# Half-size products summed in PSUM by TensorE, with ScalarE copies between, in the first layer's projection of a two-layer encoder

## The reference, cut to what matters

```python
hmod = rms_norm(x, norm_pre) * (1.0 + scale) + shift
u = jnp.dot(hmod, w_in)
x_a, g_a, q, k, v, g_b = jnp.split(u, EVEN_SPLITS, axis=-1)
xc, new_buf = causal_dwconv(x_a, conv_buf, conv_w)          # 4 taps
h, h_last = rg_lru(xc + conv_b, h0, w_a, b_a, w_x, b_x, lam)
y_a = h * jax.nn.silu(g_a)
...                                                          # window attention gives y_b
y = jnp.dot(jnp.concatenate([y_a, y_b], axis=-1), w_out)

# rg_lru, per channel, with r and i two sigmoid gates of small block products:
log_a = -LRU_C * r * softplus(-lam);  a = exp(log_a)
gated_x = sqrt(-expm1(2.0 * log_a)) * (i * xf)
h[t] = a[t] * h[t-1] + gated_x[t]
```

## Time and profile before

| | us |
|---|---|
| median of 3 runs (lowest, highest) | 1354.24 (1353.94, 1354.58) |
| the profiled execution's own time | 1355.17 |
| its span in the trace | 1353.0 |
| TensorE busy, share of the span | 1322.2, 98% |
| VectorE busy | 847.0, 63% |
| ScalarE busy | 434.6, 32% |
| GpSimd busy | 331.3, 24% |

### The profile page before, as it was taken

The page is one execution under the profiler, slowest core; times in us unless marked ns, Lnnn a source line. Parts: engine busy times, 40 slices in busy tenths (PEclk is TensorE's granted clock), DMA queues, the critical chain, the costliest instruction groups (busy, mean ns, idle before and its releaser), DMA issues.

```text
span 1353.0 us, 28616 instructions
## 1 busy us (share of the span) xinstructions
PE 1322.2 (98%) x11800; PEld 917.9 (68%) x11800; DVE 847.0 (63%) x1940; ACT 434.6 (32%) x1044; POOL 331.3 (24%) x450
## 2 busy tenths in 40 slices
PE   5999999999999999999999999999999999999997
PEld 4677776666655554667877788877788777875543
DVE  2747874355453375684885858868588585782246
ACT  4213443344431232521423314234142241432211
POOL 1023200010013232623312323124232242212352
PEclk9999999999999999999999999999999999999999
DMA  9521006002035522121112012120121200441124
GB/s 368 231 69 36 8 33 278 1 1 79 3 131 169 195 92 100 22 73 30 69 36 68 34 36 93 38 70 35 34 85 44 74 35 33 137 149 26 44 85 169
DMA packets 63769, 112.03 MB, mean 83 GB/s; under 512 B 34832, under 2 KB 39176, under 8 KB 62104
## 3 DMA queue, kind: packets, MB, share of 16 engines
q1 hardware_dynamic: 63640, 110.21, 24.3%
HBM read 91.79 MB, written 18.40 MB: 81 GB/s over the span
## 4 chain that ended last, share of the span: by engine, by line
PE 87%; DVE 7%; DMA 3%; POOL 1%; issue 1%; ACT 1%; SPq 0%; DVEq 0%; POOLq 0%; ACTq 0%
PE psum L1136 82%; PE psum L1139 4%; DMA mem<-x 1%; DVE mem L2971 1%; DVE mem L2782 1%; DVE mem L3296 1%; DMA mem<-x_dram 1%; DMA y<-mem 0%; DVE mem L3062 0%; DVE mem L3173 0%; DVE mem L2951 0%; POOL mem L958 0%; DVE mem L2788 0%; ACT mem L2095 0%; DVE mem L3050 0%
## 5 line engine op out<-in xcount | busy, mean ns | idle before, releaser
L1136 PE MATMUL psum<-mem 32*32 32x32 f32 (+12 forms) x11216 | 1261.6, 297 | 7.3 <-DMA mem<-modw 1.4
L1136 PEld LDWEIGHTS psum<-mem 128*128 128x128 f32 (+6 forms) x11216 | 851.2, 141 | 388.3 <-issue 199.5
L2971 DVE SCALAR_TENSOR_TENSOR mem<-mem 128x576 f32<-128x576 f32 (+1 forms) x126 | 106.2, 843 | 0.0
L1139 PE MATMUL psum<-mem 128*128 128x128 f32 (+1 forms) x584 | 83.7, 281 | 16.6 <-ACT mem L1935 13.7
L1139 PEld LDWEIGHTS psum<-mem 128*128 128x128 f32 (+1 forms) x584 | 69.3, 146 | 39.1 <-issue 19.3
L2286 ACT ACTIVATE mem<-mem 128x128 f32<-128x128 f32 x72 | 22.0, 305 | 127.7 <-DVE mem L3221 74.5
L2752 DVE TENSOR_TENSOR mem<-mem,psum 128x512 f32<-128x512 f32 x28 | 19.2, 687 | 42.5 <-PE psum L1136 40.5
L1015 POOL COPY mem<-mem 128x3 f32<-128x3 f32 x24 | 8.9, 370 | 148.8 <-DVE mem L2929 71.1
L2172 ACT ACTIVATE mem<-psum 128x288 f32<-128x288 f32 x28 | 11.4, 407 | 104.0 <-PE psum L1136 104.0
L2064 ACT ACTIVATE mem<-mem 128x256 f32<-128x256 f32 x72 | 35.5, 495 | 26.4 <-DVE mem L2705 26.4
L2182 ACT ACTIVATE mem<-mem 128x576 f32<-128x576 f32 (+1 forms) x42 | 32.7, 779 | 28.0 <-DVE mem L2949 28.0
(11 more groups left out here) (260 smaller groups left out, 1268.1 us busy)
## 6 DMA issues: line engine op xcount, KB each, us to landing
mem<-modw SPq DMA_DIRECT2D x12, 2048.0 KB, 11.2
mem<-w SPq DMA_DIRECT2D x44, 512.0 KB, 4.4
mem<-x SPq DMA_DIRECT2D x10, 512.0 KB, 4.6
x_dram<-mem SPq DMA_DIRECT2D x9, 512.0 KB, 2.9
mem<-row_dram SPq DMA_DIRECT2D x8, 576.0 KB, 5.0
mem<-x_dram SPq DMA_DIRECT2D x9, 512.0 KB, 3.7
mem<-wout SPq DMA_DIRECT2D x1, 4096.0 KB, 15.1
mem<-gs SPq DMA_DIRECT2D x8, 512.0 KB, 3.6
```

What stands on the lines that cost most here:

```text
L1136: return pe.matmul(*a, **k)
L1139: return pe.transpose(out, in_, ident[0:n, 0:n])
L2971: x = dve.scalar_tensor_tensor(cvm, U1[:, m, lo + j:hi + j], CW[:, 3 * g + ORDER[m], j:j + 1], cvm, ALU.mult, ALU.add)
```

## The change

The seven products and their operands stay. What changes is where they are added, who empties the banks, and in which order the engines of the loop come to it:

- The products are made in the order 1, 2, 6, 5, 7, 4, 3. Products 1, 6, 7 and 4 accumulate in one bank (`start` is false for 6, 7 and 4), products 5 and 3 in bank 4 or 5, and product 2 stands alone.
- ScalarE copies the running sum out after each of 1, 6, 7 and 4 (p1, u2, u3, c21): 8 copies in a pair in place of 2. TensorE adds the next product onto a bank only after the copy. u2, u3, u4 and c21 are no longer VectorE's work; c11, c22 and c12 stay, 6 instructions in a pair in place of 14.
- On VectorE the whole convolution of the next tile, and c11, stand ahead of the wait for the square root; c22 stands between the last product and the scan; the gates of c12 stand at the head of `chain`.
- On ScalarE the two tanh of c12 stand at the head of the turn, ahead of the six tanh that empty banks 6 and 7; the copies of p1 stand ahead of the exponential, those of u2 ahead of the square root, those of u3 and c21 between the tanh of the gates.

The diff's core:

```diff
-STEP = {"1": 0, "6": 2, "2": 4, "7": 6, "5": 8, "4": 10, "3": 12}
+STEP = {"1": 0, "2": 2, "6": 4, "5": 6, "7": 8, "4": 10, "3": 12}
+ADD, ADDS0 = {"c11": 0, "c22": 2, "c12": 4}, 6
+COPY, COPIES0 = {"p1": 0, "u2": 2, "u3": 4, "c21": 6}, 8
 def pair_bank(p, step):
-    return 2 * ((ROLE[step] + p) % 3)
+    return 4 if step in "53" else 2 * (1 - p % 2) if step == "2" else 2 * (p % 2)
...
# TensorE, pair
-                               start=(k == 0), stop=(k == HALF - 1))
+                               start=(k == 0 and step in "125"), stop=(k == HALF - 1),
+                               skip_group_check=(step in "6743"))
...
                 for j in range(2):
+                    pe.wait_ge(sem("st_cp"), copied_to(p, "p1", j))
                     part("6", j, S2, 0, T2, 0, lo(j))
                 for j in range(2):
+                    if p:
+                        pe.wait_ge(sem("st_add"), added_to(p - 1, "c12", j))
...
+                    part("5", j, w2, 0, T1, 0, lo(j))
                 for j in range(2):
-                    pe.wait_ge(sem("st_cp"), 2 * p + j + 1)
+                    pe.wait_ge(sem("st_cp"), copied_to(p, "u2", j))
                     part("7", j, S3, 0, T3, 0, lo(j))
...
                 for j in range(2):
-                    pe.wait_ge(sem("st_add"), STEPS * p + ADD["c11"] + j + 1)
+                    pe.wait_ge(sem("st_cp"), copied_to(p, "u3", j))
                     part("4", j, w2, HALF, T4, 0, lo(j))
                 pe.wait_ge(sem("s_made"), 4 * p + SUMS["s4"])
                 for j in range(2):
-                    pe.wait_ge(sem("st_add"), STEPS * p + ADD["u3"] + j + 1)
+                    pe.wait_ge(sem("st_add"), added_to(p, "c22", j))
                     part("3", j, S4, 0, HT, HALF, hi(j))
...
# ScalarE, lru
+                if m:
+                    gate_tanh(m - 1, "c12", U2c)
                 for i in range(6):
                     wait(act, sem("l_mm"), 6 * m + i + 1)
...
+                if m < LM - 1:
+                    copied(m + 1, "p1")
                 c.mark(act.activation(la, tr, ACT.Exp, ...))
                 act.activation(lw_, tr, ACT.Tanh, ...).then_inc(sem("l_a"), 1)
                 if m < LM - 1:
-                    copied(m + 1)
-                if m:
-                    gate_tanh(m - 1, "c12", U2c)
+                    copied(m + 1, "u2")
                 wait(act, sem("l_w"), m + 1)
...
-                for name, src in (("c11", P1c), ("c22", V22), ("c21", U3c)):
-                    gate_tanh(m, name, src)
+                gate_tanh(m, "c11", P1c)
+                copied(m + 1, "u3")
+                gate_tanh(m, "c22", V22)
+                copied(m + 1, "c21")
+                gate_tanh(m, "c21", U3c)
...
# VectorE, added, chain and lru
-            ADDS = {"u2": (P1c, U2c, "cp"), "c11": (P1c, P1c, "cp"), "u3": (U2c, U3c, "u2"),
-                    "c22": (U3c, V22, "u3"), "u4": (U2c, U2c, "u2"), "c21": (U3c, U3c, "u3"),
-                    "c12": (U2c, U2c, "u4")}
+            ADDS = {"c11": (P1c, "p1"), "c22": (V22, "u3"), "c12": (U2c, "u2")}
...
                 for j in range(2):
                     dve.wait_ge(sem("st_mm"), STEPS * p + STEP[FROM[name]] + j + 1)
+                    dve.wait_ge(sem("st_cp"), copied_to(p, after, j))
...
+                if m:
+                    gates(m - 1, "c12", U2c)
                 dve.wait_ge(sem("l_a"), m + 1)
...
-                if m:
-                    gates(m - 1, "c12", U2c)
                 if m < LM - 1:
-                    added(m + 1, "u2")
+                    conv0(m + 1)
+                    added(m + 1, "c11")
                 dve.wait_ge(sem("l_sq"), m + 1)
                 c.sync()
                 c.mark(dve.scalar_tensor_tensor(lg, ti, 0.5, lw_, ALU.mult, ALU.mult))
+                if m < LM - 1:
+                    added(m + 1, "c22")
...
                 p = m + 1
-                added(p, "c11")
-                conv0(m + 1, 0)
-                added(p, "u3")
-                conv0(m + 1, 1)
                 gates(m, "c11", P1c)
-                added(p, "c22")
-                added(p, "u4")
                 gates(m, "c22", V22)
-                added(p, "c21")
                 gates(m, "c21", U3c)
                 dve.wait_ge(sem("g_ev"), G_PAIR * m + OUTS["c21"] + 2)
                 dve.scalar_tensor_tensor(YT[:, m], lh, 0.5, YT[:, m], ALU.mult, ALU.mult
                                          ).then_inc(sem("l_y"), 1)
                 added(p, "c12")
```

More of the change, by code:

```diff
@@ L1270, in pair @@
                 for j in range(2):
-                    freed(j, 0, "u4")
+                    if p:
+                        pe.wait_ge(sem("st_add"), added_to(p - 1, "c11", j))
+                    else:
+                        pe.wait_ge(sem("xa_ev"), j + 1)
                     part("1", j, w1, 0, HT, 0, lo(j))
+                for j in range(2):
+                    if p:
+                        pe.wait_ge(sem("st_cp"), copied_to(p - 1, "c21", j))
+                    else:
+                        pe.wait_ge(sem("xa_ev"), 2 + j + 1)
+                    part("2", j, w1, HALF, HT, HALF, lo(j))
                 pe.wait_ge(sem("s_made"), 4 * p + SUMS["s2"])
@@ L1312, in gates, with freed @@
                     pe.wait_ge(sem(f"w0_in{q}"), 16 * m + 48)
-                    project(m, q, "g_mm", lambda n: pe.wait_ge(
-                        sem("st_add"), STEPS * (PAIRS - 1) + LAST_FREE[3 * q + n]))
+                    def freed(n):
+                        j = (3 * q + n) % 2
+                        if 3 * q + n >= 4:
+                            pe.wait_ge(sem("st_add"), added_to(PAIRS - 1, "c12", j))
+                        elif 3 * q + n < 2:
+                            pe.wait_ge(sem("st_add"), added_to(PAIRS - 1, "c11", j))
+                        else:
+                            pe.wait_ge(sem("st_cp"), copied_to(PAIRS - 1, "c21", j))
+                    project(m, q, "g_mm", freed)
             tiles(LM, gates)
@@ L1954, in constants, with copied @@
                 c.mark(act.activation(ltmp[:, 0], ltmp[:, 1], ACT.Tanh))
-            def copied(p):
+            COPIED = {"p1": (P1c, "c11"), "u2": (U2c, "c12"), "u3": (V22, "c22"), "c21": (U3c, "c21")}
+            def copied(p, name):
+                dst, last = COPIED[name]
                 for j in range(2):
-                    wait(act, sem("st_mm"), STEPS * p + STEP["1"] + j + 1)
+                    wait(act, sem("st_mm"), STEPS * p + STEP[FROM[name]] + j + 1)
                     if p >= 2:
[L1961 to L1964, removed]
+                        wait(act, sem("g_ev"), G_PAIR * (p - 2) + OUTS[last] + j + 1)
+                    elif p and last in ADD:
+                        wait(act, sem("st_add"), added_to(0, last, j))
+                    if p == 0 and name == "c21":
+                        out = UA[:, 2, PRE + j * SUB:PRE + (j + 1) * SUB]
+                    else:
+                        out = dst[:, j]
+                    act.activation(out, B(pair_bank(p, FROM[name]) + j)[:, 0:SUB], ACT.Copy
                                    ).then_inc(sem("st_cp"), 1)
@@ L1988, in _ @@
                     i.then_inc(sem("xa_ev"), 1)
-            copied(0)
+            copied(0, "p1")
+            copied(0, "u2")
             constants()
+            copied(0, "u3")
+            copied(0, "c21")
             def lru(m):
@@ L2566, in _, with conv0 @@
             dve.wait_ge(sem("pool_zero"), 1)
-            def conv0(m, part=None):
+            def conv0(m):
                 if m < 2:
@@ L2662, in _ @@
             added(0, "c22", UA[:, 2])
-            added(0, "u4")
-            added(0, "c21", UA[:, 2])
             added(0, "c12", UA[:, 3])
```

61 lines of the change are left out of this document (22 added, 39 removed).

## The result

The changed kernel takes 1368.96 us (median of 4 runs, 1368.36 to 1369.57), the kernel before beside it 1354.41 (4 runs, 1353.94 to 1354.95): 14.6 us slower, ratio 1.0107 (95% interval 1.009 to 1.0125). The forecast was 1365.6 in a range of 1359.5 to 1369.5; direction and place were right, and 3.4 us were missing. The result lies 0.5 us under the top of the range.

The account below looks back on a forecast made before the run. TensorE, busy 98%, was taken to bound the kernel, so only its waits count. Stalls of 4.7 + 4.7 + 2.0 = 11.4 us on 1355.17 give 1366.6, less 0.9 for the median: 1365.6, range 1359.5 to 1369.5.

Parts of the forecast that it names:

- The bound and the free parts: Loop: only TensorE's waits count; reordered products, fewer VectorE additions and extra ScalarE copies were put at nothing.
- The tight copy: ScalarE's copy of u3 between products 7 and 4: ends at 21.7, 1.5 us to spare, no cost.
- The deciding step: Turn's head: c12's tanh, waiting for VectorE, delays the six bank-freeing tanh; TensorE waits 2.0 us in each of three turns.
- Scans wait for GpSimd: Turns 0 and 1: VectorE's scans wait out GpSimd's sums, 2.7 us, making the stall 4.7 us.
- Rival A: Scans do not wait for GpSimd: stalls of 2.0 each, 6.0 to 8.0 in all, 1360.2 to 1362.2 us; chance 0.22.
- the meeting with S4: Turns 0 and 1: GpSimd's fourth sum falls on VectorE's gates, where VectorE waits for ScalarE anyway; no cost.
- the sum: Stalls of 4.7, 4.7 and 2.0, 11.4 us in all, added to the profiled execution: 1366.6, as median 1365.6 us.
- rival B: TensorE's clock falls in the stalls: up to 1.6 us for each of three, 1367.2 to 1370.4 us; chance 0.17.
- that dip: Kernel before, 28 to 32 us: TensorE busy 2.67 of 4, then mean clock 0.60 for 4 us, 1.6 us given up.
- C: Nothing is seen: VectorE's tail is 2 us shorter, floor of 0.6 remains, 1354.8 us; chance 0.06.
- D: Faster: relieved VectorE lets ScalarE free banks at once in the gate matmuls, 0.6 a turn, 1351.9 us; chance 0.02.
- E: New wait inside the pair: ScalarE late for u3's copy, 1 to 2 us a turn, 1369 to 1372 us; chance 0.05.

Follow-up runs that it names:

- the kernel with both causes removed: Changed kernel with c12's tanh and gates moved behind the exponential and GpSimd's sums held back behind l_y: 1353.81 us against 1355.32 for the kernel before, ratio 0.9989.
- the first two experiments: Two separate edits of the changed kernel: c12's tanh and gates behind the exponential, 1358.0 us; GpSimd's sums of pairs 2 and 3 held back behind l_y, 1358.4 us.

## Why the prediction was right, and where it was short

**The bound and the free parts held.** TensorE's products in another order cost nothing, and neither did the copies between them: the kernel with both causes removed runs the loop in exactly the old time. The tight copy, u3 between 7 and 4, was no wait anywhere.

**The deciding step held, and nearly its size.** c12's tanh at the head of ScalarE's turn waits for the addition that VectorE makes last. Forecast stalls 4.7, 4.7 and 2.0; measured 4.95, 4.95 and 1.76. The scan starts 24.1 us behind the mark (129.03 - 104.93), forecast 24.0. Undoing the step removes 11.6 of 14.6 us, the slow clock included; making it alone in the kernel before costs 6.0.

**Scans wait for GpSimd: right, with one term mis-sized and one wrongly left out.** Rival A is refuted. The scans lost 2.4 us, not 2.7 (0.4 in the long one, 2.0 in the short ones, beside L828 and L830 and not L826 and L828 as I had named them). But I let the meeting with S4 cost nothing, "where VectorE waits for ScalarE anyway": the gates of c22 took 1.88 us instead of 0.83 in turn 0, and ScalarE's next tanh waited for them. The two make 3.4 us, of which 3.2 reach the mark, against 2.7; the stall without sums was 1.76 and not 2.0, so the two errors partly cancel. The Trainium skill, "SBUF — State Buffer", section "Who interferes with whom", says that a VectorE instruction with two SBUF inputs contends with a GpSimd instruction that reads SBUF. The runs of this case agree for scans: 5.93 us beside sums, 3.54 without.

**The step that fell short is the sum: rival B came true beside the forecast, not in its place.** The granted clock went to half in both long stalls (in the first about 2 us behind TensorE's last matmul, in the second only at its end) and cost 1.65 and 1.35 us, 3.0 in all. I had called a stall of 4.7 us "deeper than that dip", yet put B at 0.17 as if it excluded the forecast. 11.66 us of stalls and 3.0 make the 14.66 of the loop, where the forecast had 11.4 and nothing for the clock. B was a consequence of the forecast, and the likeliest time should have held both: 1365.6 and my own 1.6 for each long stall, 1368.8. That 1.6 came so close is in part luck, for with c22 behind the scan a stall of 3.92 us cost 2.3 to 2.6. I read it from a dip early in the kernel, and in the profile of after the same stretch does not dip: TensorE is busy 1.94 us of the 4 at 28 to 32, less than before, and the clock of the next 4 us is 1.00. It is luck, too, that the range held the result, since only the room left for B brought it to 1369.5. The Trainium skill, "TensorE: Matmul & The Clock Gate", section "HAM oscillation — how this bites in real kernels", describes waits between bursts of matmuls after which the engine starts at half rate. The two long stalls of after agree; the short one of 1.76 us kept its clock at 1.00.

Rivals C, D and E did not occur. Of D, though, something was there: the 0.6 us of waiting in each turn's gate matmuls is real time, and other matmuls between them cover it. The way to it was not a prompter ScalarE, as D had it.

**What stays open.** The loop accounts for the total in after by the medians (14.66 of 14.6), but most of the others end lower than their loops say: 3.0 for 3.7, 3.4 for 5.2, 10.7 for 13.3 with c22 behind the scan, and -1.5 for 0.0 with both causes removed. By the profiled spans after does so too, 13.7 for 14.66. In the profiled executions part lies ahead of the loop, where the first mark comes between 104.5 and 105.1 us in different kernels, and up to 1.0 in the last stage, whose code is the same: before, the chain of waits there runs over output stores and loads, in after, and in most of its variants, it is TensorE alone. I have no run that tells why. It is why the gain of the version with both causes removed, 0.1%, is not claimed as a gain of the accumulation, and why 1.8 us, not 3.0, is what interleaving is shown to win in turns 0 to 2.

## What to carry to other kernels

An instruction that waits for another engine's last work of a turn must not stand ahead of the instruction that frees the bounding engine's buffers, on a queue that runs in order: move it behind, where its result is first needed. When work is taken from a helper, look at when its last result comes, not at how busy it is: VectorE became less busy (837 us for 847) and later: its additions of c12 end 36.2 us behind the mark of turn 0 for 32.8 before. And price a stall together with the clock that follows it.

## What the runs showed of the hardware

TensorE's clock after idling, with its rows: in after TensorE is idle for 4.95 us ahead of turn 1 (137.16 to 142.11), the clock is at 0.50 from about 139.3, and stays there until about 146 us. Ahead of turn 2 it is idle as long, and the clock falls only at about 180.2, just before TensorE starts again at 180.33:

```profile
178.00:180.00 2.00, 0.00 (x0) 0.00 (x0) 1.85 (x5) 0.99 (x3) 0.00 (x0) 1.00 0.11 45
180.00:182.00 2.00, 1.67 (x3) 1.06 (x4) 0.31 (x1) 0.75 (x2) 0.00 (x0) 0.56 0.00 0
```

So with stalls of one length the fall came at different times. In the kernel before with c12's tanh moved alone, the second stall, 3.05 us long, was followed by:

```profile
172.00:176.00 4.00, 3.03 (x5) 1.77 (x6) 0.00 (x0) 2.03 (x6) 0.00 (x0) 0.62 0.17 68
```

The stall of 1.76 us ahead of turn 3 of after, and stalls of 1.74 to 1.86 us in the first two experiments, left it at 1.00; what lies between 1.9 and 3.05 us these runs do not settle. The lowered clock cost 1.35 to 1.65 us a stall in after and in the one of 3.05 us, and 2.27 and 2.55 in the run with c22 behind the scan: the price did not go by the stall's length. Repeating matmuls that had to be done anyway kept it up and was worth 3 us.

A scan of VectorE and a GpSimd operation that read SBUF shut each other out whole: eight short scans of 0.16 us each took 3.26 us beside two sums, and in the kernel before with TensorE interleaved 4.46 beside three. That is about 1.0 to 1.1 us for each sum let in; the forecast had 1.1.
